# One 512-column product in place of two 256-column ones in the feed-forward layers of a two-block transformer kernel

## The reference

```
def swiglu(x, w_in, w_out):
    a, b = jnp.split(x @ w_in, 2, axis=-1)
    return (jax.nn.silu(a) * b) @ w_out
...
    x = x + 0.5 * swiglu(rmsnorm(x, ffn1_norm[l]), w_ffn1_in[l], w_ffn1_out[l])
...
    x = x + 0.5 * swiglu(rmsnorm(x, ffn2_norm[l]), w_ffn2_in[l], w_ffn2_out[l])
```

## Time and profile before

| | |
|---|---|
| median of 3 runs | 2747.86 us (2746.77 to 2748.28) |
| the profiled execution | 2747.19 us |
| its span, first to last instruction | 2745.4 us |
| mean granted TensorE clock | 0.996 of full speed |
| matmuls | 21952 |

### The profile page before, as it was taken

The page is one execution under the profiler, slowest core; times in us unless marked ns, Lnnn a source line. Parts: engine busy times, 40 slices in busy tenths (PEclk is TensorE's granted clock), DMA queues, the critical chain, the costliest instruction groups (busy, mean ns, idle before and its releaser), DMA issues.

```text
span 2745.4 us, 51059 instructions
## 1 busy us (share of the span) xinstructions
PE 2688.4 (98%) x21952; PEld 2569.7 (94%) x21952; DVE 1834.1 (67%) x3008; ACT 1303.7 (47%) x1867; POOL 73.1 (3%) x70
## 2 busy tenths in 40 slices
PE   8999999999999999999999999999999999999998
PEld 8999899999999889999999888799999998888997
DVE  5678666666676776767666547766666754776665
ACT  5445544444444555444544335544454433554443
POOL 0000100000000010000000001100000000110000
PEclk9999999999999999999999999999999999999999
DMA  7554466556556355555564654455555565444653
GB/s 268 185 177 128 139 181 195 189 188 198 194 173 185 108 169 185 174 195 188 192 208 161 198 140 128 119 175 197 188 177 190 176 202 147 139 107 160 199 189 104
DMA packets 481376, 474.60 MB, mean 173 GB/s; under 512 B 47104, under 2 KB 464512, under 8 KB 481024
## 3 DMA queue, kind: packets, MB, share of 16 engines
q1 hardware_dynamic: 477568, 460.85, 52.9%
q0 software_dynamic: 3584, 10.49, 1.4%
HBM read 465.01 MB, written 6.29 MB: 172 GB/s over the span
## 4 chain that ended last, share of the span: by engine, by line
PE 84%; DVE 9%; ACT 4%; issue 2%; DMA 1%; DVEq 0%; SPq 0%; ACTq 0%
PE ps L1070 31%; PE ps L971 30%; PE ps L1091 16%; DVE WL L1927 2%; PE ps L1132 2%; ACT WH L1541 2%; PE ps L1177 1%; DVE REGION L2082 1%; PE ps L1018 1%; DVE MX L2089 1%; DVE REGION L2115 1%; PE ps L1022 1%; PE ps L1213 1%; PE ps L1014 0%; DVE U L1891 0%
## 5 line engine op out<-in xcount | busy, mean ns | idle before, releaser
L1927 DVE TENSOR_TENSOR WL<-RAW,WH 128x2048 fp32r<-128x2048 f32 (+2 forms) x390 | 871.8, 2241 | 459.7 <-ACT WH L1541 457.8
L1541 ACT ACTIVATE WH<-RAW 128x2048 fp32r<-128x2048 f32 (+2 forms) x398 | 737.6, 1867 | 149.4 <-DMA RAW<-in_w_in 77.0
L1091 PE MATMUL ps<-HH,WH 128*128 128x256 f32 x1408 | 388.6, 276 | 0.0
L1091 PE MATMUL ps<-HH,WL 128*128 128x256 f32 x1408 | 388.6, 276 | 0.0
L1091 PE MATMUL ps<-HL,WH 128*128 128x256 f32 x1408 | 388.6, 276 | 0.0
L971 PE MATMUL ps<-UH,WH 128*128 128x256 f32 x1328 | 376.6, 284 | 2.5 <-DVE WL L1927 2.5
L971 PE MATMUL ps<-UL,WH 128*128 128x256 f32 x1328 | 368.8, 278 | 0.0
L971 PE MATMUL ps<-UH,WL 128*128 128x256 f32 x1328 | 367.6, 277 | 0.0
L1070 PE MATMUL ps<-UH,WH 128*128 128x256 f32 x2688 | 363.2, 277 | 1.3 <-DVE WL L1927 1.1
L1070 PE MATMUL ps<-UH,WL 128*128 128x256 f32 x2688 | 360.0, 276 | 0.0
L1070 PE MATMUL ps<-UL,WH 128*128 128x256 f32 x2688 | 359.8, 276 | 0.0
(11 more groups left out here) (334 smaller groups left out, 3633.9 us busy)
## 6 DMA issues: line engine op xcount, KB each, us to landing
RAW<-in_w_ffn_in SPq DMA_DIRECT2D x88, 1024.0 KB, 5.1
RAW<-in_ffn_wi SPq DMA_DIRECT2D x88, 1024.0 KB, 5.0
RAW<-in_w_in SPq DMA_DIRECT2D x86, 1024.0 KB, 5.3
RAW<-in_w_ffn_out SPq DMA_DIRECT2D x32, 1024.0 KB, 5.1
RAW<-in_ffn_wo SPq DMA_DIRECT2D x32, 1024.0 KB, 5.1
RAW<-in_w_out SPq DMA_DIRECT2D x16, 1024.0 KB, 5.2
RAW<-in_w_ffn_out SPq DMA_DIRECT2D x16, 768.0 KB, 4.4
RAW<-in_ffn_wo SPq DMA_DIRECT2D x16, 768.0 KB, 4.4
```

Source lines behind the costliest of these rows:

```text
L1091: last = nc.tensor.matmul(bank(n + side, 0, T), a[:, k, side * P:(side + 1) * P], b[:, k0 + k, :], start=k0 + k == 0 and a is wh and b is ...
L1541: nc.scalar.activation(split_ap(s, part_high(s)), raw_ap(s), ACT.Copy).then_inc(weights_high, 1)
L1927: v_.tensor_tensor(split_ap(s, part_low(s)), raw_ap(s), split_ap(s, part_high(s)).bitcast(FP), ALU.subtract)\
```

## The change

`UH` and `UL` become two halves of one tile `UHL`, `HH` and `HL` of one tile `HHL`, at the same addresses. In the up products of the first matrix and in all products of the second, `WH` is loaded once and streams the high and the low activation as one matmul of 512 columns over the whole PSUM bank: the first 256 columns collect `WH`·high and `WL`·high, the other 256 collect `WH`·low. Gate products, `opening`, `product_first` and everything outside the feed-forward parts stay.

VectorE adds the two halves with a reduction over the bank. For an up product that takes the place of `scaled`, and the norm's factor is left out there; it is multiplied in behind the second matrix, where `add_halves_to_x` has three instructions, each waiting for the one ahead, in place of the one of `add_to_x`.

```
+            def onto_both(n, a, both, start=False, stop=False):
+                return nc.tensor.matmul(bank(n).rearrange("p (h t) -> p h t", h=2), a, both, start=start, stop=stop)
...
+                        onto_both(n, wh[:, 0, cols], UHL[:, :, 0, :], start=True)
+                        for k in range(DK):
+                            nc.tensor.matmul(bank(n, 0, T), wl[:, k, cols], UH[:, k, :], start=False, stop=False)
+                        for k in range(1, DK):
+                            last = onto_both(n, wh[:, k, cols], UHL[:, :, k, :], stop=k == DK - 1)
...
-                                for a, b in ((wh, HH), (wl, HH), (wh, HL)):
-                                    last = nc.tensor.matmul(bank(n + side, 0, T), a[:, k, side * P:(side + 1) * P], b[:, k0 + k, :],
-                                                            start=k0 + k == 0 and a is wh and b is HH, stop=k0 + k == FK - 1 and b is HL)
+                                if k0 + k == 0:
+                                    onto_both(n + side, wh[:, k, cols], HHL[:, :, 0, :], start=True)
+                                last = nc.tensor.matmul(bank(n + side, 0, T), wl[:, k, cols], HH[:, k0 + k, :], start=False, stop=False)
+                                if k0 + k:
+                                    last = onto_both(n + side, wh[:, k, cols], HHL[:, :, k0 + k, :], stop=k0 + k == FK - 1)
...
+            def halves_sum(dst, n):
+                return v_.reduce_sum(dst, bank(n).rearrange("p (h t) -> p t h", h=2), AX.X)
+            def add_halves_to_x(name, m):
+                n = first[name] + m
+                part = TMP[:, m % 2, 0:T]
+                wait_product(dve, n)
+                link(halves_sum(part, n))
+                link(v_.tensor_tensor(part, part, RSTD[:], ALU.mult))
+                v_.scalar_tensor_tensor(X[:, m, :], part, 0.5, X[:, m, :], ALU.mult, ALU.add).then_inc(evicted[n % BANKS], 1)
+                wait_evicted(dve, n)
+                add_squares(m)
...
+                def joined(dst, n):
+                    wait_product(dve, n)
+                    halves_sum(dst, n).then_inc(evicted[n % BANKS], 1)
...
-                    scaled(TMP[:, 0, 0:T], n)
+                    joined(TMP[:, 0, 0:T], n)
                     feed.to(s0 + 2 * j + 3)
-                    scaled(TMP[:, 1, 0:T], n + 1)
+                    joined(TMP[:, 1, 0:T], n + 1)
...
-                        add_to_x(name + ".out", 0.5, m)
+                        add_halves_to_x(name + ".out", m)
```

More of the change, by code:

```diff
@@ L482, in build @@
         gap("GAP_U", MOVING)
-        UH, UL = sb("UH", [P, DK, T], FR), sb("UL", [P, DK, T], FR)
+        UHL = sb("UHL", [P, 2, DK, T], FR)
+        UH, UL = UHL[:, 0], UHL[:, 1]
         gap("GAP_W", STILL)
@@ L533, in build @@
             high.append(overlay(f"WH{i}", [P, SLOT], at + SLOT + APART))
-        HH, HL = overlay("HH", [P, FK, T], 0), overlay("HL", [P, FK, T], FK * T)
+        HHL = overlay("HHL", [P, 2, FK, T], 0)
+        HH, HL = HHL[:, 0], HHL[:, 1]
         OTH, OTL = overlay("OTH", [P, 4, T], 2 * DK * T), overlay("OTL", [P, 4, T], TAIL + 80)
@@ L1067, in ffn @@
                         wait_room(pe, n)
[L1068 to L1071, removed]
+                        cols = slice(side * P, (side + 1) * P)
+                        if j % 2 == 0:
+                            for i, (a, b) in enumerate(((wh, UH), (wl, UH), (wh, UL))):
+                                for k in range(DK):
+                                    last = nc.tensor.matmul(bank(n, 0, T), a[:, k, cols], b[:, k, :],
+                                                            start=i == 0 and k == 0, stop=i == 2 and k == DK - 1)
+                            last.then_inc(product_done, 1)
+                            continue
+                        onto_both(n, wh[:, 0, cols], UHL[:, :, 0, :], start=True)
+                        for k in range(DK):
+                            nc.tensor.matmul(bank(n, 0, T), wl[:, k, cols], UH[:, k, :], start=False, stop=False)
+                        for k in range(1, DK):
+                            last = onto_both(n, wh[:, k, cols], UHL[:, :, k, :], stop=k == DK - 1)
                         last.then_inc(product_done, 1)
```

## The result

The changed kernel takes **2797.13 us** (median; 2796.68 to 2802.72), the kernel before 2747.7 us: 1.0185 times as long, with an interval of 1.0167 to 1.0203. The forecast was 2730.5 us. The profiled span went from 2745.4 to 2795.3 us, 49.9 us more.

The account below looks back on a forecast made before the run. PE, busy 98% of the span, was taken as the bound, its weight loads setting the matmul pace. 2747.2 - 30.4 (merged pairs) + 13.3 (ends) = 2730.1 us for the profiled execution; forecast 2730.5 us, range 2724 to 2737.

Parts of the forecast that it names:

- a weight load takes some 113 ns of its own and just sets the pace of the 256-column matmuls: On PE: the load, not the column stream, was said to make the 113.3 ns of each 256-column matmul.
- the 215.8 ns: Predicted pace of a 512-column split matmul on PE, taken from the spacing of 256-column unsplit float32 matmuls.
- the 214.2 ns of the unsplit rows: Cost of 256 more unsplit columns on PE, halved to predict 108.7 ns for 256 split columns with 1.6 ns fixed cost.
- A term of -30.4 us: Feed-forward products on PE: 2816 merged pairs, each 215.8 instead of 226.6 ns, 10.8 ns less.
- lower bound: Merged pairs on PE: if the excess stays once per matmul, 220.4 ns each and 17.5 us gained.
- The matmul with low weights between them keeps 113.3 ns: On PE: the next matmul's load still has only those 256 columns to hide under, so no change.
- The ends: Ends of feed-forward parts: longer evictions, 1.17 to 1.18 us more each, stall PE at six ends, 13.3 us more.
- nothing for VectorE inside the stages: First and second matrices: VectorE's longer evictions stay hidden as it still keeps up, 12.5 of 14.5 us; cost nothing.
- The rival of a slow reduction: Reduction at the ends takes 1.38 us instead of 0.69, stalls 21.6 us, time 2739 us; chance 0.12.
- Only the fixed cost is saved: Excess comes with every 256 split columns on PE: 225.0 ns for 512, gain 4.5 us, time 2757 us; chance 0.07.
- break-even: The change makes the kernel slower once a 512-column matmul on PE takes more than 221.9 ns.
- gap rule: Warm PE gap N/2.4 + 2.5 ns: a merged pair saves 2.5 ns, 7 us in all, kernel 6 us slower.

Follow-up runs that it names:

- experiment 5: Kernel before, with the feed-forward product of high weights and low activation moved to second place and cut to 128 columns: 2764.40 us, 1.0062.
- experiment 4: Changed kernel with halves side by side, long matmuls cut to 384 columns and VectorE evicting as before: 2680.52 us in one run.
- experiment 7: Kernel before, no 512-column matmul, with the activations' tiles and the region moved by 64 B: 2797.49 us, 1.0188.
- 3: Changed kernel with high and low activation side by side, so that 512 columns are one run of addresses: 2797.99 us, 1.0184.
- 8: Changed kernel with VectorE evicting one bank half as before, and feed-forward weights in the first three buffers only: 2920.77 us in one run.
- 2: Also called the second kernel: PE as in the changed kernel, VectorE evicting only one bank half as before, without the reduction: 2772.95 us, 1.0095.
- experiment 1: Changed kernel with only each product's first row tile as a 512-column matmul, the others two of 256 on reloaded weights: 2794.28 us, 1.0173.
- experiment 9: Kernel before, with two more linked VectorE instructions at each eviction of an output product, PE unchanged: 2761.91 us, 1.0051.
- experiment 11: Changed kernel with X of both last tiles updated before squares and low parts, except in the part ending at 1335 us: 2788.20 us, 1.0149.

## Why the prediction was wrong

**The step that failed** is the reading at the end of the first part, "a weight load takes some 113 ns of its own and just sets the pace of the 256-column matmuls", and the 215.8 ns that hung on it. The load does take 112 ns (experiment 5; the 125 ns that the prediction read in the earlier trace rows was a mean over a pause). But the stream of 256 split columns takes 113.3 ns too (experiment 4), so with the load gone 512 columns still take 226.6. The error was made in halving the 214.2 ns of the unsplit rows. Those stream for about twice as long over 256 columns, and I took half of that, 0.418 ns a column, to be what a split column needs. It isn't: a split column takes 0.4427 ns, 6% more. The 215.8 ns with which the prediction said a rule to agree for 512 columns was a row of 256 unsplit columns too. The durations in the earlier trace rows, 276 and 380 ns, could not tell the two apart. A term of -30.4 us becomes 0. Its lower bound, 17.5 us of gain, failed with it: it too let a 512-column stream pay the excess once.

**What the prediction had not priced** is that the stages get slower, by 29.1 us in the two traces. Of this the 512-column matmuls, at 230.6 and 231.8 ns in the mean instead of 226.6, are 1408 x (4.0 + 5.2) = 13.0 us, and the low-weight ones, at 118.3 and 117.6 instead of 113.3, are 1408 x (5.0 + 4.3) = 13.1 us; 3.0 us are left for the gate products around them, whose form did not change. "The matmul with low weights between them keeps 113.3 ns" was wrong by these 4 to 5 ns. That a slower step of this size exists without long matmuls is shown (experiment 7), and so is, for the first matrices, that it hangs on where the weights lie against the activations; that the jump, the use of buffers 3 to 5 or the reduction makes it is excluded (3, 8, 2). Through what the changed products bring it about stays open: their length at each step is not needed, since experiment 1 has nearly the same stages with one long matmul for each product, and the two halves of the bank do not do it alone. A run without that last long one, or with the new order of matmuls and one half of the bank, was not made. I read the step as a load and a stream at the same memory at the wrong moment, which is argued and not shown.

**The ends** came as said, and the clock made them worse. The reduction took 685 ns (690 forecast), the eviction 1.64 us (1.62), and the waits for that tile grew by 18.4 - 6.2 = 12.2 us against 13.3. By ends it was less even than forecast: 1.5 us at 852, where 2.36 was said, and 3.0 us at 199 (waits of 0.53 and 1.27 us before, 2.32 and 2.46 after). Not foreseen was the clock behind them. Four new stretches of 3.4 us stand at these ends, 13.7 us; elsewhere there is 3.4 us less than before, which no experiment ties to the change. That is 10.2 us more at half the rate, 5.1 us lost by an estimate of half of it. The second kernel puts the whole price of the eviction at 24.2 us. Waits (18.4 - 4.7 = 13.7 us more than in that kernel) and clock (5.1) give 19 of it, the stages 2.5 (935.5 and 491.3 us there, against 937.9 and 491.4), and some 3 I can't place. So the prediction's nothing for VectorE inside the stages held to within these 2.5 us. The rival of a slow reduction fell with its 685 ns.

**The rivals.** *Only the fixed cost is saved*, at 0.07, was right that the excess comes with every 256 split columns; its reason, moving operand and weight being read side by side, no run shows. It had 225.0 ns and 2757 us, 40 us short, since it too priced neither the slower stages nor the clock. By its own break-even, 221.9 ns, the change was lost. The Trainium skill's gap rule ("TensorE: Matmul & The Clock Gate", section "Back-to-back issue gap"), N/2.4 + 2.5 ns, stood beside this rival and led to the right sign with wrong distances: by it 109.2, 162.5 and 215.8 ns for 256, 384 and 512 columns. Measured were 113.3, 170 and 226. For 256 I had seen the gap between rule and row, and explained it away by the load instead of reading it as 6% on each column. The measurement decides: for split operands the rule is too short by an amount that grows with the columns.

In sum: 2747.2 + 0 + 29.1 + 12.2 + 5.1 = 2793.6 us, against 2797.1 for the profiled execution (49.9 above 2747.2); 3.5 us stay unplaced.

## What to carry to other kernels

Fewer weight loads are worth something only where the columns stream faster than the loads come; two limits can lie some 1% apart (112 and 113.3 ns here), and the way to tell is one run with shorter streams and one with longer ones, not rows of another operand type. Where matmuls run back to back at the least distance, hold every change of form or layout against it: 49 us over 21952 matmuls, 2.2 ns each in the mean, cost as much as the whole change (experiment 7). And a longer eviction matters just at a stage's last tiles, where giving PE its operand before all side work brought back 8.9 of the 24.2 us that the eviction costs.

## What the runs showed of the hardware

Split float32 columns stream at 0.4427 ns each, for 256, 384 and 512 columns (fastest clusters around 113.3, 170 and 226 ns), with no fixed part to be seen, and loads of 128 columns come 112 ns apart. With the activations and the region moved by 64 B in their partitions, matmuls whose weights did not move along come 118 to 119.6 ns apart in the first matrices, those whose weights did 113.3 to 114.4, and the kernel is 1.9% slower. The granted clock stood at half for 3.4 us behind waits of PE of 2.4 to 2.5 us at four ends of the changed kernel, and behind two of 2.14 and 2.05 us in experiment 9; that cost 1.4 us on the sixteen matmuls in it. It did not fall behind the wait of 1.01 us in experiment 11. Nor did it fall behind every long wait: the one of 1.47 us at 686.84 and that of 2.25 us at 2264 in the changed kernel were followed by sixteen matmuls in 2.04 us.
